# A row scale moved from a copy on ScalarE into the matmul that turns x

## The reference

```
h = rmsnorm(x, n_pre_mix);  proj = h @ w_in
... four mixers (gated delta, dilated window, stick-breaking, retention), each gated, summed
mixed = (g_a*y_a + g_b*y_b + g_c*y_c + g_d*y_d) @ w_o
x = x + rmsnorm(mixed, n_post_mix)
h2 = rmsnorm(x, n_pre_mlp)
x = x + rmsnorm(square(relu(h2 @ w_mlp_in)) @ w_mlp_out, n_post_mlp)

rmsnorm(x, w) = x * rsqrt(mean(x*x, -1) + 1e-6) * w
```

## Time and profile before

| | us |
|---|---|
| median of 3 runs | 2480.09 (2478.93 to 2480.55) |
| the profiled execution | 2480.09 |
| its span | 2478.3 |
| TensorE busy | 2389.3 (96%) |
| VectorE, ScalarE, GpSimd busy | 970.5, 783.6, 1318.4 |

### The profile page before, as it was taken

The page is one execution under the profiler, slowest core; times in us unless marked ns, Lnnn a source line. Parts: engine busy times, 40 slices in busy tenths (PEclk is TensorE's granted clock), DMA queues, the critical chain, the costliest instruction groups (busy, mean ns, idle before and its releaser), DMA issues.

```text
span 2478.3 us, 29728 instructions
## 1 busy us (share of the span) xinstructions
PE 2389.3 (96%) x11872; PEld 1953.2 (79%) x11872; DVE 970.5 (39%) x1396; ACT 783.6 (32%) x1549; POOL 1318.4 (53%) x748
## 2 busy tenths in 40 slices
PE   8999999999998999999999999999999989999998
PEld 7798877787776788888887888777777767888887
DVE  3663324444544441123256532254355345311223
ACT  5433326213125241122254342352231352311221
POOL 5512663555552556677655126546555425666774
PEclk9999999999999999999999999999999999999999
DMA  4300321322230233322222013213222202333221
GB/s 156 91 26 27 94 85 51 102 85 85 62 90 28 94 91 97 94 97 98 86 77 85 18 35 95 84 52 111 82 89 63 80 29 93 103 95 100 95 94 68
DMA packets 107672, 197.45 MB, mean 80 GB/s; under 512 B 8592, under 2 KB 21008, under 8 KB 107152
## 3 DMA queue, kind: packets, MB, share of 16 engines
q1 hardware_dynamic: 106384, 189.27, 24.8%
q10 hardware_dynamic: 1152, 6.29, 0.7%
HBM read 193.44 MB, written 2.10 MB: 79 GB/s over the span
## 4 chain that ended last, share of the span: by engine, by line
PE 84%; DVE 9%; ACT 5%; issue 2%; POOL 0%; DMA 0%; POOLq 0%; DVEq 0%; SPq 0%; ACTq 0%
PE big L1609 62%; PE mix L1609 8%; PE mix L1746 5%; PE big L1922 1%; DVE c_lo L1394 1%; PE mix L1890 1%; PE mix L1816 1%; PE mix L1989 1%; ACT scr L986 1%; PE mix L2080 1%; PE mix L1901 1%; PE mix L1709 1%; DVE scr L1241 0%; DVE scr L1406 0%; ACT o_hi L595 0%
## 5 line engine op out<-in xcount | busy, mean ns | idle before, releaser
L558 POOL TENSOR_SCALAR ring_hi<-stage 128x1024 fp32r<-128x1024 f32 (+2 forms) x372 | 383.2, 1030 | 1103.7 <-PE big L1609 1044.1
L560 POOL TENSOR_TENSOR ring_lo<-stage,ring_hi 128x1024 fp32r<-128x1024 f32 (+2 forms) x372 | 936.7, 2518 | 31.1
L1609 PE MATMUL big<-h_hi,ring_hi 128*128 128x512 f32 (+1 forms) x1904 | 725.5, 381 | 10.5 <-DVE h_lo L1126 6.3
L1609 PE MATMUL big<-h_hi,ring_lo 128*128 128x512 f32 (+1 forms) x1904 | 715.2, 376 | 0.0
L1609 PE MATMUL big<-h_lo,ring_hi 128*128 128x512 f32 (+1 forms) x1904 | 715.0, 376 | 0.0
L1609 PEld LDWEIGHTS big<-h_hi,ring_hi 128*128 128x128 f32 x1904 | 358.6, 188 | 84.6 <-issue 7.7
L1609 PEld LDWEIGHTS big<-h_lo,ring_hi 128*128 128x128 f32 x1904 | 358.4, 188 | 66.1
L1609 PEld LDWEIGHTS big<-h_hi,ring_lo 128*128 128x128 f32 x1904 | 358.8, 188 | 64.6 <-issue 1.9
L1609 PE MATMUL big<-ring_hi,h_hi 128*128 128x512 f32 x448 | 176.6, 394 | 14.0 <-DVE scr L1173 11.8
L1557 DVE TENSOR_TENSOR h_lo<-scr,h_hi 128x1024 fp32r<-128x1024 f32 x64 | 84.8, 1325 | 249.2 <-ACT h_hi L1044 249.2
L1609 PE MATMUL big<-ring_hi,h_lo 128*128 128x512 f32 x448 | 175.4, 391 | 0.0
(11 more groups left out here) (255 smaller groups left out, 2948.5 us busy)
## 6 DMA issues: line engine op xcount, KB each, us to landing
stage<-in_w_in SPq DMA_DIRECT2D x168, 512.0 KB, 3.5
stage<-in_w_mlp_in SPq DMA_DIRECT2D x64, 512.0 KB, 3.6
stage<-in_w_mlp_out SPq DMA_DIRECT2D x64, 512.0 KB, 3.3
stage<-in_w_o SPq DMA_DIRECT2D x16, 512.0 KB, 3.3
stage<-in_w_br_a SPq DMA_DIRECT2D x8, 512.0 KB, 3.8
stage<-in_w_br_c SPq DMA_DIRECT2D x8, 512.0 KB, 3.3
stage<-in_w_br_d SPq DMA_DIRECT2D x8, 512.0 KB, 3.3
stage<-in_w_br_b SPq DMA_DIRECT2D x8, 512.0 KB, 3.7
```

What stands on the lines that cost most here:

```text
L558: nc.gpsimd.tensor_scalar(rH[jw][0:pp, r, 0:kk, 0:job.n], w, 1.0, 0.0, ALU.mult, ALU.add).then_inc(sem("w_hi"), 1)
L560: nc.gpsimd.tensor_tensor(rL[jw][0:pp, r, 0:kk, 0:job.n], w, f32(rH[jw][0:pp, r, 0:kk, 0:job.n]), ALU.subtract).then_inc(sem("w_ready"), 1)
L1609: ins_ = MM(o_, a_, r_, start=s0, stop=s1)
```

## The change

- Step 3 is gone. In its place VectorE multiplies the identity with y, which gives a diagonal tile of 128x128 (`diagonal`, into the new view `turn`), and TensorE computes `x_block.T @ diagonal` with an ordinary f32 matmul where it transposed before. A tile's eight matmuls wait for one semaphore.
- On ScalarE `split_hi` of the last four feature tiles stands in one piece after the root, where it was in two pieces of two around it.
- The two Newton operations and the two variance additions use scalar_tensor_tensor in place of tensor_scalar with two operands by pointer.
- At the start: `small()` (the norm weights) is issued ahead of the first weights; ScalarE squares tile 2 before the root of tile 1; VectorE makes the diagonal of tile 0 before the variance of tile 1; tiles 2 and 3 are turned after aq's unit 1 in place of unit 2.

```diff
             def x_root(tag, t): ...
-            def normed(tag, t):
-                act.wait_ge(*upto(f"{tag}_nw", 2 * t + 2))
-                for hf in range(2):
-                    cs = slice(hf * 512, hf * 512 + 512)
-                    A(hn[:, t, cs], xv[:, t, cs], ACT.Copy, scale=p_y[:, t:t + 1]).then_inc(sem(f"{tag}_h"), 1)
...
                     x_square(name, t, ntag)
-                    if t:
-                        split_hi(ntag, nw, t - 1, (4, 5))
                     x_root(ntag, t)
                     if t:
-                        split_hi(ntag, nw, t - 1, (6, 7))
-                    normed(ntag, t)
+                        split_hi(ntag, nw, t - 1, range(4, 8))
...
+            def diagonal(tag, t):
+                newton(p_y, p_t, p_h, tag, t)
+                TS(turn[:, t, :], ident, p_y[:, t:t + 1], None, ALU.mult).then_inc(sem(f"{tag}_dg"), 1)
...
-                TS(w, y, y, h, ALU.mult, ALU.mult).then_inc(sem(f"{tag}_nw"), 1)
+                STT(w, y, y, h, ALU.mult, ALU.mult).then_inc(sem(f"{tag}_nw"), 1)
...
             def turned(tag, t):
+                pe.wait_ge(*upto(f"{tag}_dg", t + 1))
                 for hf in range(2):
                     ps = tile_of((tag, t, hf))
-                    pe.wait_ge(*upto(f"{tag}_h", 2 * t + hf + 1))
                     for q in range(4):
                         k = 4 * hf + q
-                        i = TR(ps[:, q * P:(q + 1) * P], hn[:, t, k * P:(k + 1) * P], ident)
+                        i = MM(ps[:, q * P:(q + 1) * P], xv[:, t, k * P:(k + 1) * P], turn[:, t, :], start=True, stop=True)
                     done(i, (tag, t, hf))
...
-            halves("aq", "pre1", {(0, 0): (2,), (2, 0): (3,)} if l else {(2, 2): (2, 3)})
+            halves("aq", "pre1", {(0, 0): (2,), (2, 0): (3,)} if l else {(1, 2): (2, 3)})
```

More of the change, by code:

```diff
@@ L387, in hybrid_kernel @@
         fT = sview(0, FF // P)
-        hn = scr[:, MB:MB + 4096].rearrange("p (t d) -> p t d", t=NT)
+        turn = sview(MB, NT, P)
+        x_junk = scr[:, MB + 512:MB + 512 + DM]
         postw = scr[:, FF // P * S + 2048:FF // P * S + 2048 + DM]
@@ L522, in sync_layer @@
                 token_tile(1)
+                small()
             for u, (job, i) in enumerate(UNITS):
                 if l == 0 and u in (1, 2):
-                    if u == 1:
-                        small()
                     token_tile(u + 1)
@@ L674, in scalar_layer @@
                 x_root("pre1", 0)
+                first_square(2)
                 x_root("pre1", 1)
-                normed("pre1", 0)
-                normed("pre1", 1)
                 act.wait_ge(*upto("small_loaded", 16))
@@ L680, in scalar_layer @@
                 split_hi("pre1", LN1, 1)
-                first_square(2)
                 first_square(3)
[L683 to L688, removed]
+                x_root("pre1", 2)
+                x_root("pre1", 3)
+                split_hi("pre1", LN1, 2)
+                split_hi("pre1", LN1, 3)
             def conv_raw(i):
@@ L1078, in y_variance @@
                 dve.wait_ge(*upto(f"{tag}_ss", NT + t + 1))
-                TS(n_v[:, t:t + 1], n_ss[:, t:t + 1], EPS, n_ss[:, NT + t:NT + t + 1], ALU.add, ALU.add).then_inc(sem(f"{tag}_v"), 1)
+                STT(n_v[:, t:t + 1], n_ss[:, t:t + 1], EPS, n_ss[:, NT + t:NT + t + 1], ALU.add, ALU.add).then_inc(sem(f"{tag}_v"), 1)
                 dve.wait_ge(*upto(f"{tag}_v", t + 1))
-                TS(n_h[:, t:t + 1], n_v[:, t:t + 1], -0.5, None, ALU.mult).then_inc(sem(f"{tag}_half"), 1)
+                TS(n_h[:, t:t + 1], n_v[:, t:t + 1], -0.5, None, ALU.mult).then_inc(sem(f"{tag}_nw"), 1)
             def newton(v_y, v_t, v_h, tag, t):
@@ L1086, in newton @@
                 dve.wait_ge(*upto(f"{tag}_y", t + 1))
-                dve.wait_ge(*upto(f"{tag}_half", t + 1))
-                TS(w, y, y, h, ALU.mult, ALU.mult).then_inc(sem(f"{tag}_nw"), 1)
-                dve.wait_ge(*upto(f"{tag}_nw", 2 * t + 1))
-                TS(y, w, 1.5, y, ALU.add, ALU.mult).then_inc(sem(f"{tag}_nw"), 1)
-                dve.wait_ge(*upto(f"{tag}_nw", 2 * t + 2))
+                dve.wait_ge(*upto(f"{tag}_nw", 3 * t + 1))
+                STT(w, y, y, h, ALU.mult, ALU.mult).then_inc(sem(f"{tag}_nw"), 1)
+                dve.wait_ge(*upto(f"{tag}_nw", 3 * t + 2))
+                STT(y, w, 1.5, y, ALU.add, ALU.mult).then_inc(sem(f"{tag}_nw"), 1)
+                dve.wait_ge(*upto(f"{tag}_nw", 3 * t + 3))
             def y_weighted(name, hf, t, tag):
@@ L1145, in after_products @@
                     x_variance(ntag, t)
-                    newton(p_y, p_t, p_h, ntag, t)
+                    diagonal(ntag, t)
                     if t:
@@ L1208, in vector_layer @@
             if l == 0:
+                dve.wait_ge(ident_loaded, 16)
                 x_variance("pre1", 0)
                 dve.wait_ge(x_loaded[1], 16)
-                STT(hn[:, 1, :], xv[:, 1, :], 1.0 / DM, xv[:, 1, :], ALU.mult, ALU.mult,
+                STT(x_junk, xv[:, 1, :], 1.0 / DM, xv[:, 1, :], ALU.mult, ALU.mult,
                     accum_out=p_ss[:, 2:3]).then_inc(sem("x_ss1"), 1)
+                diagonal("pre1", 0)
                 x_variance("pre1", 1)
-                newton(p_y, p_t, p_h, "pre1", 0)
-                newton(p_y, p_t, p_h, "pre1", 1)
+                diagonal("pre1", 1)
                 split_lo("pre1", LN1, 0)
@@ L1219, in vector_layer @@
                     x_variance("pre1", t)
-                    newton(p_y, p_t, p_h, "pre1", t)
+                    diagonal("pre1", t)
                 for t in (2, 3):
```

10 lines of the change are left out of this document (4 added, 6 removed), and 8 rows, old and new, of the table PER_LAYER.

## The result

The changed kernel takes 2506.37 us (median of four runs, 2502.30 to 2506.84) against 2479.97 for the kernel before on the same chip: a ratio of 1.0103, 95% interval 1.0086 to 1.0120. The forecast was 2485.5. The profiled execution took 2504.55 us, its span is 2502.7 where it was 2478.3: 24.4 us more, where the sum had 5.4. The time lies above the whole range of the forecast, 2482.5 to 2487.9.

What follows compares the result with a forecast made beforehand. TensorE, busy in 96% of the span, was taken as the bound. Seams +2.4 and +1.9, start +1.3 and end -0.15 summed to +5.4 us on 2480.09: 2485.5, range 2482.5 to 2487.9.

Steps and rivals of the forecast that it cites:

- Small operations: VectorE's one-element steps: about 0.05 us less each as scalar_tensor_tensor, at four places of a tile's chain; added diagonal 0.25 us.
- Price of a turned tile: TensorE: eight matmuls by the diagonal take 1.78 us where eight transposes take 0.87, +0.91 a tile, 14.6 for 16 tiles.
- Rival 1: TensorE's matmul by a diagonal costs what a transpose costs, so only waits go: 2474 us, faster; chance 5%.
- The seams and the start: Places where x is turned: +2.4 us for two o1 to up0 seams, +1.9 at dn1 to aq, +1.3 at the start.
- o1 to up0: Seam in each layer: two tiles at +0.91, up0 starting 0.65 us earlier; net +1.2 each, bounds -0.4 to +1.8.
- dn1 to aq: Seam passed once: 1.7 us of waits for the copy go, 3.65 added; net +1.9, bounds +1.5 and +3.65.
- the start: Kernel's start: aq 0.5 us later, tiles 2 and 3 +1.8, earlier clock rise -1.0; net +1.3, bounds +0.4 and +2.4.
- the end: Last tile's chain after 2471.6 holds three of the cheaper small steps: -0.15 us.
- a new wait for the diagonal appears in front of L1655: Sign that the forecast is wrong: a new wait ahead of TensorE's turning matmuls, whose diagonals were expected in time.
- the 16.5 named there: Sign that the forecast is wrong: aq starting past 16.5 us, where about 15.8 was expected.

Runs made afterwards that it cites:

- e3_both: Changed kernel with the four small VectorE steps as tensor_scalar again and the diagonal made by ScalarE; 2480.49 us, ratio 1.0009.
- e4_before_stt: Kernel before with only the four small steps written as scalar_tensor_tensor, copies and transposes kept; 2491.20 us, ratio 1.0045.
- p16: Kernel before with 16 transposes that nothing reads in TensorE's wait ahead of aq in layer 0; 2480.53 us (one run).
- p16b: The kernel before with the same 16 unread transposes ahead of aq, timed once more; 2477.50 us (eleven runs), ratio 0.9988.
- e5_transpose: Kernel of both edits (small steps as tensor_scalar, diagonal on ScalarE) with transposes instead of real matmuls, factor y left out; 2483.24 us, ratio 1.0003.

## Why the prediction was wrong

**The step that failed is "Small operations".** It priced the scalar_tensor_tensor steps at 0.05 us less and the diagonal at 0.25, bounded by rows of other shapes or other operands. All those rows were durations of VectorE undisturbed, and what VectorE waits for inside an instruction was put at nothing without a reason. GpSimd is busy for 53% of the span and the two small steps sit where it splits the next weights. The steps measured up to 1.78 and 0.98, the diagonal up to 2.47. The kernel e3_both takes this away (by moving the diagonal to ScalarE) and 20.1 of the 25.1 us with it; e4_before_stt puts only the small steps in and pays 14.3 at the same places (+2.45, +4.20, +3.71, +4.10, -0.15; 11.7 by the medians).

**Price of a turned tile: right.** Thirty-two records from 26.39 on take 3.74 us, so (3.74 - 0.27)/31 = 0.112 a record and 0.224 a matmul; 0.223 was forecast, and two records each:

```profile
26.39 3.74 PE L1655 MATMUL mix<-scr,x_sb 128*128 128x128 f32 x32
```

Rival 1, that it costs what a transpose does, is refuted: the transposes took 0.109 each.

**The seams and the start: right but for the failed step.** With nothing standing (e3_both) the terms came out as +1.07 and +1.28 at o1 to up0 (forecast +1.2 each), +1.58 at dn1 to aq (+1.9), +1.04 at the start (+1.3), 0.00 at the end (-0.15; the small steps there are back to what they were): 5.0 in sum, 5.4 forecast. (The upper bound of the start, +2.4, is 2.3 by its own terms, 0.5 + 1.8; tile 2's square, put at 9.45, began at 9.62 in e3_both and at 10.21 in after, when its transfer had landed.) In the changed kernel they were +7.67 and +7.64, +4.34, +5.60 and -0.20. The seam of layer 0 can be followed to the end: up0's first matmul is 3.71 us later than before, the seam's own start 0.43 later, so +3.28 where I had -0.65; two tiles more +1.82; and the lower level, 12 matmuls at 0.213 instead of 0.12 (1.1) and sixteen records in 3.34 instead of 1.95 (1.4). Together 7.6 of the 7.67. The 2.5 of the clock (1.1 and 1.4) are a second term that my sum did not have: I asked where the clock would rise earlier and not where a longer gap would lower it.

**What I listed as making it wrong** was the right list: "a new wait for the diagonal appears in front of L1655", and it did, 3.50 us at the start. But no rival gave it a price, so the range ended at 2487.9. aq also started past the 16.5 named there, at 20.0.

**The mixers.** I took the rest of the kernel as fixed, and that was a second weakness of the sum: without the standing instructions the time would have come out at 2480.49 (e3_both), under the lower end of my range, with the terms of the seams and the start nearly right. In twelve executions, of eleven kernels, that do the same mixer work, the two stages together took 1632.9 to 1640.9 us. p16 and p16b are the same kernel, and their first stage took 818.59 and 821.90, the second 820.69 and 815.46. The difference goes with the clock around gaps of TensorE inside a stage. About half of it is at one near 115 us, first in p16, then in p16b:

```profile
110.00:120.00 10.00, 6.67 (x34) 5.58 (x33) 7.84 (x12) 1.32 (x3) 2.33 (x2) 0.91 0.19 54
120.00:130.00 10.00, 10.00 (x62) 8.86 (x61) 8.70 (x11) 2.62 (x6) 3.72 (x2) 0.92 0.18 53
```

```profile
110.00:120.00 10.00, 6.66 (x30) 5.73 (x30) 7.21 (x10) 1.32 (x3) 2.25 (x1) 0.77 0.20 54
120.00:130.00 10.00, 10.00 (x57) 8.76 (x57) 8.54 (x10) 1.86 (x5) 3.75 (x2) 0.89 0.18 53
```

TensorE is idle 3.3 us in the first ten of each, and the granted clock is 0.91 and then 0.92 in the one, 0.77 and then 0.89 in the other. The other half follows a gap near 790 us: from 805 to 815 the granted clock is 1.00 in p16 and 0.83 in p16b. Summed over the first stage, (1 - granted clock) times the length of each 5 us stretch is 11.95 and 15.35, a difference of 3.4 for the 3.3 between the stages. By the table this is why a local gain of 4.6 us did not show in e5_transpose's profile. It is also the likely reason, not shown, why the kernel before itself ranged from 2475.61 to 2484.62 in one series of runs. What decides it in an execution stays open; that it is the execution and not the kernel is shown only by the one pair, and p16b's stages (821.90 and 815.46) are those of before (821.94 and 815.42) to 0.04 us.

## What to carry to other kernels

Before a VectorE instruction is added or rewritten, look at what GpSimd does at that moment: "cheaper by 0.05 us" held only where it did not overlap one of GpSimd's instructions, and of the one-column forms with both tensors in SBUF, tensor_scalar with its operands by pointer was the one that never stood here. Take one-element steps of a critical chain as they are until the rows beside them are read, not only the rows of the same form. And price a longer wait twice, once as the wait and once as the lower clock behind it; cut the trace at landmarks, so that a local gain isn't judged by a total that moves by itself.

## What was not expected of the hardware

- A VectorE instruction with two tensor inputs in SBUF, or a 128x128 tensor_scalar, that begins inside a GpSimd instruction stands until that one's end: 2.15 to 2.28 us beside a 2.34 us subtraction, 0.85 to 0.98 beside a 1.04 us rounding, where each takes 0.15 to 0.28 alone. With one of its inputs in PSUM it takes 0.15 (128x1) and 0.28 (128x128), as it does alone. Beside a memset of 0.95 us only the 128x128 tensor_scalar stood (0.80).
- Transposes alone brought TensorE to the higher level: the seventeenth to thirty-second of them took 0.12 us each on average ((2.07 - 0.27)/15), the first sixteen at 0.215.
- Filling a wait with work that nothing reads made the kernel faster, by 1.6 us at the start.
